# Attention: probabilities by values as split float32r products, value halves side by side, output taken out in two halves a tile

## What is computed

```python
logits = jnp.einsum('bqgrd,bqkgd->bqgrk', qg, k_sel).astype(jnp.float32) * (HD ** -0.5)
logits = jnp.where(valid[:, :, None, None, :], logits + bias, -jnp.inf)
p = jax.nn.softmax(logits, axis=-1)
out = jnp.einsum('bqgrk,bqkgd->bqgrd', p.astype(v.dtype), v_sel)
```

## Time and profile before

| | |
|---|---|
| timed runs | 1722.30, 1722.75, 1731.42 us; median 1722.75 us |
| profiled execution, its own time | 1721.74 us |
| span of its instructions | 1719.8 us |
| mean granted TensorE clock | 0.97 |
| attention stage in the span | 555 to 753 us |

### The profile page before, as it was taken

The page is one execution under the profiler, slowest core; times in us unless marked ns, Lnnn a source line. Parts: engine busy times, 40 slices in busy tenths (PEclk is TensorE's granted clock), DMA queues, the critical chain, the costliest instruction groups (busy, mean ns, idle before and its releaser), DMA issues. The chain is left out here.

```text
span 1719.8 us, 23441 instructions
## 1 busy us (share of the span) xinstructions
PE 1606.1 (93%) x8496; PEld 1388.1 (81%) x8496; DVE 806.0 (47%) x1631; ACT 637.9 (37%) x1312; POOL 456.1 (27%) x401
## 2 busy tenths in 40 slices
PE   5997899999998699979979999999999999999996
PEld 4985677777676578967758999999999999999995
DVE  2367687888875365533333232323323233232337
ACT  3466575766456466642232110111111111111112
POOL 2211354545440321113223201222221022222206
PEclk9998999999999799989989999999999999999998
DMA  6210311111102622035323001111110111111015
GB/s 198 65 47 13 95 47 33 47 46 34 44 22 71 127 69 54 14 119 181 134 75 98 26 24 49 49 49 49 49 49 4 45 49 49 49 49 49 1 37 195
DMA packets 110928, 107.61 MB, mean 63 GB/s; under 512 B 45784, under 2 KB 93304, under 8 KB 110712
## 3 DMA queue, kind: packets, MB, share of 16 engines
q1 hardware_dynamic: 110704, 106.29, 20.3%
q10 hardware_dynamic: 136, 0.20, 0.1%
HBM read 87.09 MB, written 19.38 MB: 62 GB/s over the span
## 5 line engine op out<-in xcount | busy, mean ns | idle before, releaser
L2100 ACT ACTIVATE rf<-up 128x768 f32<-128x768 f32 x48 | 39.0, 813 | 629.7 <-PE up L304 629.7
L302 PE MATMUL up<-aT_hi,wu_hi 128*128 128x384 f32 x768 | 258.3, 336 | 3.8 <-POOL wu_lo L2152 3.8
L304 PE MATMUL up<-aT_hi,wu_lo 128*128 128x384 f32 x768 | 258.2, 336 | 0.0
L303 PE MATMUL up<-aT_lo,wu_hi 128*128 128x384 f32 x768 | 258.0, 336 | 0.0
L2201 DVE CAST fT_hi<-rf 128x768 fp32r<-128x768 f32 x48 | 30.7, 639 | 418.0 <-ACT rf L2102 418.0
L304 PE MATMUL dn<-wd_hi,fT_lo 128*128 128x512 f32 x576 | 225.0, 391 | 0.0
L303 PE MATMUL dn<-wd_lo,fT_hi 128*128 128x512 f32 x576 | 224.9, 390 | 0.0
L302 PE MATMUL dn<-wd_hi,fT_hi 128*128 128x512 f32 x576 | 224.1, 389 | 0.9 <-DVE fT_lo L2203 0.9
L2156 POOL TENSOR_TENSOR wu_lo<-raw,wu_hi 128x2048 fp32r<-128x2048 f32 x15 | 69.5, 4636 | 583.8 <-ACT wu_hi L2089 583.8
L2211 DVE TENSOR_TENSOR acc<-dn,acc 128x1024 f32<-128x1024 f32 x135 | 164.9, 1222 | 109.4 <-PE dn L304 109.4
L302 PE MATMUL rt_pj<-w_hi,aT_hi 128*128 128x512 f32 x360 | 154.0, 428 | 1.0 <-PEq L337 1.0
(11 more groups left out here) (244 smaller groups left out, 2962.2 us busy)
## 6 DMA issues: line engine op xcount, KB each, us to landing
raw<-in_w_up SPq DMA_DIRECT2D x16, 1024.0 KB, 5.6
raw<-in_w_down SPq DMA_DIRECT2D x16, 1024.0 KB, 4.9
w_raw<-in_w_in SPq DMA_DIRECT2D x36, 256.0 KB, 3.3
ob_mix<-mix_scratch SPq DMA_DIRECT2D x9, 512.0 KB, 4.1
h_scratch<-ob_h SPq DMA_DIRECT2D x9, 512.0 KB, 2.8
raw<-h_scratch SPq DMA_DIRECT2D x9, 512.0 KB, 4.2
out<-acc SPq DMA_DIRECT2D x9, 512.0 KB, 2.9
scores<-in_x_prompt SPq DMA_DIRECT2D x8, 512.0 KB, 5.8
```

The costliest lines, as they stand in the source:

```text
L302: nc.tensor.matmul(out, lhs[0], rhs[0], start=first, stop=False)
L303: nc.tensor.matmul(out, lhs[0], rhs[1], start=False, stop=False)
L304: return nc.tensor.matmul(out, lhs[1], rhs[0], start=False, stop=last)
L2100: nc.scalar.activation(rf[:, b], up[b][:, :, 0:GT], ACT.Relu).then_inc(relued, 1)
```

## The change

- The values are split once: `vparts` holds for each key block and each of the two value heads the high half (64 columns, ScalarE) and the low half (64 columns, GpSimd) side by side. ScalarE does this behind the first exponential, when the values have arrived, and GpSimd behind the first near table.
- ScalarE's copy of turned probabilities now writes a float32r high part, and VectorE gets a new step, `lower_probs(u - 2)` behind `logits(u)`, which writes the low part. The bank in `tp` comes free behind VectorE's step (`p_lo`), and so does the product.
- A product by values is two float32r instructions with different stationary operands: high probabilities by both halves of the values (128 columns), low probabilities by the high half (64 columns).
- The results of a head take 128 columns of `po`, so four heads fill the bank. VectorE takes them out twice a tile: copy the high half to `po_sum`, add the low half, multiply by the reciprocals; each waits for the one before. This stands at the start of VectorE's iterations with u % 4 == 3, and the first product of each half tile waits for it on TensorE. The reciprocals are taken in halves as well, at u % 4 == 0, and ScalarE's wait for them is relaxed accordingly.
- `pT` and `vparts` lie in the memory of `aT`, which is free in this stage.

```diff
+        pT = [x[:, 0:3 * 512].rearrange("p (b n) -> p b n", b=3) for x in spare]
+        vparts = spare[0][:, 3 * 512:3 * 512 + 2 * PT * P].rearrange("p (t g k d) -> p t g k d", t=PT, g=KV, k=2)
+        po_sum = sb("po_sum", [P, 4, HD])
...
             def exps(u):
...
-                if h == 0 and t >= 1:
-                    act.wait_ge(rd_done, t)
+                if h % 4 == 0 and t >= 1:
+                    act.wait_ge(rd_done, 2 * (t - 1) + h // 4 + 1)
...
-                    nc.scalar.activation(pT[:, n % 3, 0:w], bank_of("probs", n)[:, 0:w],
-                                         ACT.Copy).then_inc(p_kept, 1)
+                    nc.scalar.activation(pT[0][:, n % 3, 0:w], bank_of("probs", n)[:, 0:w],
+                                         ACT.Copy).then_inc(p_hi, 1)
...
+                if u == 0:
+                    act.wait_ge(v_in, 32)
+                    nc.scalar.activation(vparts[:, :, :, 0], vt[:].rearrange("p t (g d) -> p t g d", g=KV),
+                                         ACT.Copy).then_inc(v_hi, 1)
...
+            def out(t, g):
+                done = 2 * t + g
+                dve.wait_ge(rd_done, done + 1)
+                dve.wait_ge(pv_done, first_turn[HEADS * t + 4 * g + 4])
...
+                parts = po[:].rearrange("p (m k d) -> p m k d", m=4, k=2)
+                nc.vector.tensor_copy(po_sum[:], parts[:, :, 0]).then_inc(po_added, 1)
+                dve.wait_ge(po_added, 2 * done + 1)
+                nc.vector.tensor_tensor(po_sum[:], parts[:, :, 1], po_sum[:], ALU.add).then_inc(po_added, 1)
+                dve.wait_ge(po_added, 2 * done + 2)
+                nc.vector.tensor_tensor(oa[:, t % 2, 256 * g:256 * g + 256].rearrange("p (m d) -> p m d", m=4),
+                                        po_sum[:], repeated(rden[:, 4 * g:4 * g + 4], 2, HD),
+                                        ALU.mult).then_inc(oa_done, 1)
+
+            def lower_probs(u):
+                for n in range(first_turn[u], first_turn[u + 1]):
+                    dve.wait_ge(p_hi, n + 1)
+                    w = P * turns[n][2]
+                    nc.vector.tensor_tensor(pT[1][:, n % 3, 0:w], bank_of("probs", n)[:, 0:w],
+                                            pT[0][:, n % 3, 0:w].bitcast(F32), ALU.subtract).then_inc(p_lo, 1)
...
-            for u in range(NU + 3):
+            for u in range(NU + 4):
+                if u % 4 == 3 and u >= 7:
+                    out(*divmod(u // 4 - 1, 2))
                 for n in queries_at(u):
                     lower_queries(n)
                 if u < NU:
                     logits(u)
-                if u % HEADS == 0 and u:
-                    invert(u // HEADS - 1)
+                if 2 <= u < NU + 2:
+                    lower_probs(u - 2)
+                if u % 4 == 0 and 0 < u <= NU:
+                    invert(*divmod(u // 4 - 1, 2))
...
-                if u % HEADS == 2 and u > HEADS:
-                    out(u // HEADS - 1)
...
+                if t == 0:
+                    pool.wait_ge(v_hi, 1)
+                    nc.gpsimd.tensor_tensor(vparts[:, :, :, 1], vt[:].rearrange("p t (g d) -> p t g d", g=KV),
+                                            vparts[:, :, :, 0].bitcast(F32), ALU.subtract).then_inc(v_lo, 1)
...
-            readers = dict(keys=k_kept, logits=s_lg, probs=p_kept, turned=s_kept, out=s_o)
+            readers = dict(keys=k_kept, logits=s_lg, probs=p_lo, turned=s_kept, out=s_o)
...
-                if h == 0 and t >= 1:
-                    pe.wait_ge(oa_done, t)
+                if h % 4 == 0 and u >= 4:
+                    pe.wait_ge(oa_done, 2 * t + h // 4)
                 for n in range(first_turn[u], first_turn[u + 1]):
                     _, k0, m = turns[n]
-                    pe.wait_ge(p_kept, n + 1)
+                    pe.wait_ge(p_lo, n + 1)
                     for k in range(m):
...
+                        nc.tensor.matmul(po[:, c:c + P], pT[0][:, n % 3, keys],
+                                         vparts[:, k0 + k, g].rearrange("p k d -> p (k d)"),
+                                         start=(k0 + k == 0), stop=False)
+                        mm = nc.tensor.matmul(po[:, c:c + HD], pT[1][:, n % 3, keys], vparts[:, k0 + k, g, 0],
+                                              start=False, stop=(k0 + k == t))
```

More of the change, by code:

```diff
@@ L188, in hybrid_layer_kernel @@
         clear_semaphores()
-        attention_block(nc, a, sem, ident, aq_d, akT, score, toep_d, bias, bias_s, mix, ck_pf, cv_pf, cv_s)
+        attention_block(nc, a, sem, ident, aT, aq_d, akT, score, toep_d, bias, bias_s, mix, ck_pf, cv_pf, cv_s)
         phase_a.close()
@@ L1334, in _, with attention_block @@
                         scores(i - 2)
-def attention_block(nc, a, sem, ident, aq_d, akT, mask, toep_d, bias, bias_s, mix, ck_pf, cv_pf, cv_s):
+def attention_block(nc, a, sem, ident, aT, aq_d, akT, mask, toep_d, bias, bias_s, mix, ck_pf, cv_pf, cv_s):
     NU = PT * HEADS
@@ L1354, in attention_block @@
         pr = sb("probs", [P, 3, D])
-        pT = sb("pT", [P, 3, 512])
+        spare = [x[:].rearrange("p c t -> p (c t)") for x in aT]
+        pT = [x[:, 0:3 * 512].rearrange("p (b n) -> p b n", b=3) for x in spare]
+        vparts = spare[0][:, 3 * 512:3 * 512 + 2 * PT * P].rearrange("p (t g k d) -> p t g k d", t=PT, g=KV, k=2)
+        po_sum = sb("po_sum", [P, 4, HD])
         mx = sb("mx", [P, 3, HEADS])
@@ L1376, in attention_block @@
         neg_done, exp_done = sem("at_neg"), sem("at_exp")
-        p_turned, p_kept, pv_done, rd_done = (sem(f"at_{n}") for n in ("p_turned", "p_kept", "pv", "rd"))
+        p_turned, p_hi, p_lo, pv_done, rd_done = (sem(f"at_{n}") for n in ("p_turned", "p_hi", "p_lo", "pv", "rd"))
+        v_hi, v_lo, po_added = sem("at_v_hi"), sem("at_v_lo"), sem("at_po_added")
         oa_done, oa_out = sem("at_oa"), [sem("at_oa_out0"), sem("at_oa_out1")]
@@ L1484, in _ @@
                     t = u // HEADS - 1
-                    sp.wait_ge(oa_done, t + 1)
+                    sp.wait_ge(oa_done, 2 * (t + 1))
                     sp.dma_start(mix[t * P:(t + 1) * P, 512:1024], oa[:, t % 2]).then_inc(oa_out[t % 2], 16)
@@ L1613, in logits, with invert @@
                                         ALU.mult).then_inc(neg_done, 1)
-            def invert(t):
-                dve.wait_ge(exp_done, HEADS * (t + 1))
+            def invert(t, g):
+                dve.wait_ge(exp_done, HEADS * t + 4 * g + 4)
                 if t >= 1:
[L1618 to L1623, removed]
+                    dve.wait_ge(oa_done, 2 * (t - 1) + g + 1)
+                heads = slice(4 * g, 4 * g + 4)
+                nc.vector.reciprocal(rden[:, heads], den[:, heads]).then_inc(rd_done, 1)
@@ L1765, in pv_u @@
                 if h == 0 and t == 0:
-                    pe.wait_ge(v_in, 32)
-                if h == 0 and t >= 1:
-                    pe.wait_ge(oa_done, t)
+                    pe.wait_ge(v_lo, 1)
+                if h % 4 == 0 and u >= 4:
+                    pe.wait_ge(oa_done, 2 * t + h // 4)
                 for n in range(first_turn[u], first_turn[u + 1]):
                     _, k0, m = turns[n]
-                    pe.wait_ge(p_kept, n + 1)
+                    pe.wait_ge(p_lo, n + 1)
                     for k in range(m):
[L1773 to L1776, removed]
+                        g, c = h // 4, h % 4 * P
+                        keys = slice(k * P, (k + 1) * P)
+                        nc.tensor.matmul(po[:, c:c + P], pT[0][:, n % 3, keys],
[3 more added lines that the diff above has]
+                                              start=False, stop=(k0 + k == t))
                     mm.then_inc(pv_done, 1)
```

5 lines of the change are left out of this document (2 added, 3 removed).

## The result

The changed kernel takes 1737.12 us, median of five runs (1736.29 to 1743.92), against 1723.79 for the kernel before in five runs (1722.30 to 1731.42): ratio 1.0081, 95% interval 1.0056 to 1.0107. It is slower by 0.8%, some 13 us; the forecast was 12 us and 1735. Two further measurements of the same kernel, `again` and `again_b`, gave 1.0087 (1.0059 to 1.0115) and 1.0090 (1.0058 to 1.0122). The profiled execution took 1736.78 us, its span 1735.0 us: 15.2 us more than before's span.

What follows compares the result with a forecast made beforehand. TensorE was taken to bound attention from tile 4 on, with waits counting in tiles 1 to 3 and VectorE becoming as full. Terms 6+3+3+0.7-0.9, about +12 us, gave 1735 us against the median; range 1720 to 1752.

Steps and rivals of the forecast that it cites:

- The pitch on TensorE: Products by values: 576 instructions at 0.107 to 0.115 us each, 0 to +4.6 us, taken as 0.
- Rival B: Products by values: the float32r pair runs faster because its load hides; at best -5 to -12 us, 1713 us; chance 0.06.
- VectorE's work: Attention stage: subtractions 46 to 53 us, output +2.2 us a tile; sign: VectorE's busy time up by 65 to 70 us.
- (a) Hand-over: Output bank, 15 points: the first product of each half waits for the half before; 6 us, range 3 to 13.5.
- (b) Queries: Turning of the next queries, once a tile: their low parts come late, behind low probabilities; 3 us, range 0 to 5.
- (c) Tiles 0 to 2: Short units, where VectorE's work is longer than the tile in tile 2; 3 us, range 0 to 8.
- my signs: What would show the forecast, by tile: tiles 1 to 3 longer by 2 to 4 us each, tile 7 by under 1.
- (d) The end: End of attention: nothing covers the last output; +0.7 us.
- (e): ScalarE's wait for the reciprocal, 1.7 us before, goes; counted at half, -0.9 us.
- Costed at nothing: Splitting the values on ScalarE and GpSimd, and the later release of the turned probabilities' bank: no added time.
- rival C: Attention stage: VectorE bounds it throughout, stalls uncovered; +27 us and above, to 1750 and beyond; chance 0.08.
- rival A: Attention stage: the loop absorbs VectorE's lateness, only a few hand-overs show; 0 to +6 us, 1723 to 1729; chance 0.20.

Runs made afterwards that it cites:

- halves_only: Kernel before with only the output taken out in two halves, heads 128 columns apart, float32 products kept and no low step: 1727.64 us, ratio 1.0022.
- no_low_step: Changed kernel without VectorE's subtractions; the second float32r instruction takes the high probabilities again: 1729.39 us, ratio 1.0038.
- early_release: Changed kernel with TensorE's first product of each half tile waiting for the output's addition instead of its multiplication: 1734.22 us, ratio 1.0056.
- out_late: Changed kernel with the output of a half tile placed behind the logits of its iteration instead of in front: 1805.56 us, ratio 1.0463.
- fill_12: Changed kernel with 12 identity transposes on TensorE before the first product of a half tile at five units: 1736.15 us, ratio 1.0057.
- low_step_only: Changed kernel without output halves: VectorE's subtractions kept, both float32r instructions 64 columns wide, output once a tile as before: 1739.37 us, ratio 1.0091.

## Why the prediction was right, and where not

- **The pitch on TensorE**, taken as unchanged at 0.107 to 0.115 us: right. It is 0.111, and `halves_only` and `no_low_step` agree tile by tile. Reading it from what the next product needed (0.29 us), not from the 0.06 us between two starts, was the step that mattered. Rival B falls.
- **VectorE's work**: 52.8 us of subtractions (53 forecast). The output costs 22.9 us with its reciprocals, where it was 7.1: +15.8 against 2.2 us for each of eight tiles, 17.6. The copy from PSUM took 0.41 us. These are sums over groups, 68.6 us; the page counts 59 us, probably since records of neighbours overlap, so the sign of 65 to 70 us was set too high.
- **(a) Hand-over**, 6 us, most of it at 8 points that no stream covers: right, and place by place. TensorE waits 5.6 to 7.8 us at 7 to 9 points; at u = 11, 23 and 35, forecast at 1.5, 1.3 and 0.8 us, it waits 1.79, 1.65 and 1.08. `early_release` agrees. `halves_only` (+5.3) doesn't confirm it: its waits there are 2.2 to 3.2 us, and its tile 1 has a clock of 0.90. Taking the streams as cover was what made it 6 and not 13.5. `out_late` shows that the cover was just enough: lateness of 18 us came through in full.
- **(b) Queries**, 3 us: not seen there. The wait of the turning for the queries' low parts is 3.6 us before and 1.9, 3.6 and 3.7 in the three profiles of the changed kernel. The low step shows in two other waits instead: 1.4 us for the bank that it releases, which I had put at nothing or into this term, and 0.5 us for the low parts themselves.
- **(c) Tiles 0 to 2**, 3 us: mis-sized. Tiles 1 and 2 alone grew by 9.6 us in the first profile, tile 1 by 6.6, beyond the 2 to 4 us of my signs. The premise failed: I read a clock of 1.00 in the earlier trace rows and added up durations as if the change couldn't touch it. It was low for 16 us of these two tiles. With the clock at 1.00 the same tiles take 18.0 us (`fill_12`, its filling included) and 18.7 us (`again`), 4.3 more than before; so the waits are worth some 4 us there and the clock the other 5, as far as single profiles can say.
- **(d) The end**, +0.7: it was +0.3. **(e)** ScalarE's wait for the reciprocal is gone from the list of waits, as said.
- **Costed at nothing**: right for the splitting of the values; for the bank see (b). The rows of the start, GpSimd's split of the values and TensorE still waiting for the cache:

```profile
570.83 2.34 POOL L1696 TENSOR_TENSOR aT_hi<-vt,aT_hi 128x1024 fp32r<-128x1024 f32 x1 [3.38 <-ACT aT_hi L1560]
573.13 4.52 POOL L1691 TENSOR_TENSOR near<-bias,scores 128x2048 f32<-128x2048 f32 x1
```

```profile
572.83 0.45 PE L1734 MATMUL at_tp<-ident,kp 128*128 128x128 f32 x1 [4.30 <-DMA vp<-in_cache_v]
```

- **VectorE as the bound** (rival C, and "as full as TensorE"): falls for tiles 4 to 7. They grew by 0.7 to 1.6 us only, and the subtractions alone add nothing in tile 7. VectorE isn't as full as TensorE either: it is busy for 86 to 87% of tiles 5 to 7, where the forecast was 92 to 97%. The loop absorbs VectorE's lateness there, as rival A said; it doesn't at the hand-overs and in the short units. My sign for A, that nothing grows, was too coarse: A held for the low step in the full tiles.

So the total came out right, 12 for 13 to 16 us, and part of that is luck. By tiles at full clock the waits are worth about 10 us (2.9+1.4+1.8+1.6+0.7+1.0+0.8 from the profiles where each was undisturbed, tile 1 with `fill_12`'s extra work, and +0.3 at the end), a little under my sum. The clock, for which the sum had no term, makes the other 5 of that profile's 16 us; the experiments on it put it between 1 and 6. The wide range, not the working, had room for it. That the change lowers the clock and that wider or added work on TensorE lifts it again is shown over many runs. Why the chip lowers it in one tile of one run and in another tile of the next stays open.

## What to carry over

Price an instruction by what the stream behind it needs, not by the distance of two recorded starts, and find out whether the stationary or the moving operand sets the pitch: where it is the load, narrower or split moving data brings nothing, and an instruction dropped brings nearly all of its time, as long as the engine is full. Work moved onto a half idle engine in a closed loop costs little where the bound engine's units are long, and shows where a single buffer is handed over or units are short. A full clock in the profile of before is no property of the stage: read the clock column again after every change, and keep an error for it in the range.

## What the runs showed of the hardware

- The granted clock of TensorE fell to its low level (1.2 GHz of 2.4) in tiles 1 to 7, which had the high one throughout in the profile of before, for 14 to 17 us in the changed kernel and 31 us in `low_step_only`. The stretches are 3.4 to 7 us long, one is 17 us, and in the changed kernel no wait of TensorE for VectorE in them is over 2 us. Widening products from 64 to 128 columns, at no cost in tile 7, took 17 us off the low time of whole runs (143 to 126 us) and gave tile 3 back from 27.4 to 21.2 us. Two profiles of one kernel show the low stretches in different tiles. A low stretch of 3.4 us cost 1.6 us.
- VectorE's tensor_tensor with both inputs in SBUF stood still for up to 3.4 us behind GpSimd's tensor_tensor of 4.5 us (0.42 became 3.83 us at most), while its neighbours reading PSUM, 0.42 us each, did not. The page SBUF — State Buffer of the Trainium skill ("SBUF: two separate sides") names this: such an operation and a GpSimd one that reads SBUF exclude each other for a whole instruction. The runs agree for VectorE behind GpSimd, and the other way round none of them shows it. The change brought in such an operation, the multiplication, and by its place at the start of an iteration it stayed clear of the near tables; moved by one step it met six of them.
- TensorE issued a float32 product with 64 moving columns as two instructions of 0.107 us, and float32r products with 128 or 64 moving columns as one of 0.111 us each, every one with its own load of 128 columns. A float32r product with 512 columns took 0.23 us.
